# A two-layer diffusion trunk on one core: the modulation sums of the attention loop move to the output projections

## The chip, the core and the metric

The kernel runs on one core of one Trainium2 chip. The engines that matter are TensorE (PE, with its weight loads PEld), VectorE (DVE), ScalarE (ACT), GpSimd (POOL) and SyncE (SP), which issues nearly all DMAs. The metric is the device time of the whole kernel in microseconds (us), lower is better. Kernels are compared by the median of several runs; the trace is of one profiled execution.

## The reference

x is (512, 1024): 512 latent tokens; ctx is (256, 1024): context tokens; c is one conditioning vector. Two layers follow each other, all in fp32. For each layer, the modulation is a matrix-vector product

```
mods = silu(c) @ mod_w[layer] + mod_b[layer]     # 6 x 1024 values
h    = rms_norm(x, w_pre) * (1 + scale) + shift  # shift, scale from mods
x    = x + gate * rms_norm(mixer(h), w_post)     # gate from mods
h    = rms_norm(x, w_ffn_pre) * (1 + scale2) + shift2
x    = x + gate2 * rms_norm(ffn(h), w_ffn_post)
```

The mixer of layer 0 (hybrid) is a bidirectional chunked gated DeltaNet beside grouped-query attention of 8 heads over 768 keys (256 context, 512 latent), both from one input projection, and one output projection w_out (1024 x 1024). The mixer of layer 1 (short convolution) is an input projection, a gated depthwise convolution and again a 1024 x 1024 output projection. The feed-forward part is an up projection, a depthwise convolution, a gate and a down projection. Which part of mods is needed when: the first 2 x 1024 values before the first projection; the rest of layer 0 from its output projection on; those of layer 1 from the end of layer 0's feed-forward part on, with gates and feed-forward values from layer 1's output projection on.

## The kernel before

Activations lie transposed, channels in the 128 partitions and 512 tokens in the free dimension, as eight tiles x[:, c, :]. A weight is loaded in units of 256 columns (w_raw, 1 MB, two buffers); ACT copies it to a rounded high part (w_hi, `split_hi`), DVE subtracts to get the low part (w_lo, `split_lo`), and PE multiplies three times per k tile (high x high, high x low, low x high). A unit makes two output tiles of 128 channels. Each engine has a program of its own, written out in order in one function for each; semaphores are the only link between them. Nothing is scheduled by a planner, so an engine that waits holds up everything behind it in its list.

The modulation is computed on the side. The first 16 of 96 parts of 128 come from rows of mod_w by PE. The other 80 are 40 pairs of 256 columns, numbered j = 0 to 39 (`PAIRS`). For each pair SP loads 1 MB (8 k tiles of 256, `load_mod_pair`); ACT multiplies each k tile by silu(c) in place (`products`, eight activations); GpSimd adds the eight k tiles in three steps of 1024, 512 and 256 elements (`mod_parts`); PE sums over the partitions by two products with a vector of ones (`mod_columns`), each writing one column of a PSUM bank. Pairs 0 to 11 run in the input projection, 12 to 19 in the DeltaNet stage, 20 to 39 in the attention loop, two in every three steps (`mod_block`).

The attention loop has 32 steps i (8 heads x 4 query blocks of 128) and a few more to drain. PE: scores of step i (L937, L938) into one of two pairs of PSUM banks; transposes of the probabilities of step i-2 (L911) into banks 4 and 5, the only buffer of them; then, in three of four steps, a third of the values product of an earlier head (L922 to L924). ACT: copy of the transposed probabilities (PTh, L1379), exp (prob, L1393), products. DVE: row maximum, reciprocal, normalisation, and the low part of the transposed probabilities (PTl, L1924). At i = 32 ACT waits for all 40 pairs and splits the first two units of w_out, and DVE does the same. Their loads wait for the pairs too, since w_raw and the pairs' slots (`mraw_c`) share space.

Behind the loop DVE makes all norm weights (`norm_weights`). The output projection (`out_units`, `y_units`) has four units, tiles t = 0 to 7. PE does tiles 0 and 1 with the k tiles outermost, the others one after the other. Per tile ACT squares the PSUM result (sum_y, L1418) and the weighted y (sum_z, L1420), DVE makes y = PSUM x weight (L1955), y * x (L1958) and a running sum (L1961), GpSimd adds the squares. After tiles 1, 3 and 5 ACT and DVE split the next unit but one. Tile t writes PSUM bank t mod 4. The same functions do the second output projection, in layer 1.

## Time and profile before

| | us |
|---|---|
| median of 3 runs (lowest, highest) | 1708.76 (1706.11, 1711.48) |
| the profiled execution | 1714.39 |
| its span | 1712.6 |
| PE busy in the span | 1576.1 (92%) |
| DVE busy | 873.1 (51%) |
| ACT busy | 668.5 (39%) |
| GpSimd busy | 369.5 (22%) |
| ACT's products of pairs 12 to 39 (L1234, 224 instructions) | 92.2 |

The span is the time from the first to the last instruction of the profiled execution; the execution's own time is 1.8 us longer. The attention loop lies at 524 to 672 us of it, the first output projection at 692 to 740 us, the second at 1267 to 1315 us. The mean grant of the TensorE clock over the whole execution is 0.943 of full speed. The chain of work that ended last is PE for 77% of the span, DVE 10%, ACT 6%, GpSimd 3%.

### The profile page before, as it was taken

Reading aid. Unit: us, or ns where it says so; the run is one execution under the profiler, and the core shown is the slowest. Engines: PE = TensorE matmul, PEld = TensorE weight load, DVE = VectorE, ACT = ScalarE, POOL = GpSimd, SP = SyncE. Lnnn points to the kernel's source line nnn. Section 1 sums busy time; section 2 is a strip of 40 time slices with the busy share of each in tenths; the row PEclk is TensorE's granted clock in tenths of the full one; section 3 lists DMA queues with packets and bytes.
Section 4 is the critical chain, followed back from the end, with each engine's and each line's share of the span. In section 5 each row is a group of like instructions: output and inputs, shape, how many; then the busy total and the mean of one; then the engine's idle time right before and its main releaser. Section 6 shows DMA issues by size and latency. Waiting matters only on the chain.

```text
span 1712.6 us, 19828 instructions
## 1 busy us (share of the span) xinstructions
PE 1576.1 (92%) x7752; PEld 1290.8 (75%) x7752; DVE 873.1 (51%) x1150; ACT 668.5 (39%) x1044; POOL 369.5 (22%) x255
## 2 busy tenths in 40 slices
PE   8899896669978886999999999989999999999997
PEld 2688786568965554868888888868888788888886
DVE  2654424887626676574444434464446644444222
ACT  2444536313436896224333332232233433343221
POOL 3028502346764663300000001100003000000000
PEclk9899898789985998989999999999998999999999
DMA  8325610001133453213333222213222233232231
GB/s 337 99 86 172 172 50 13 1 1 50 50 113 109 148 172 77 71 50 99 98 98 98 95 90 92 95 47 111 92 92 74 74 99 98 98 98 92 83 96 50
DMA packets 153907, 160.18 MB, mean 94 GB/s; under 512 B 11383, under 2 KB 151144, under 8 KB 152808
## 3 DMA queue, kind: packets, MB, share of 16 engines
q1 hardware_dynamic: 153344, 158.95, 28.9%
q8 instruction: 52, 0.85, 0.2%
q10 hardware_dynamic: 488, 0.18, 0.0%
q14 instruction: 23, 0.19, 0.0%
HBM read 157.03 MB, written 2.10 MB: 93 GB/s over the span
## 4 chain that ended last, share of the span: by engine, by line
PE 77%; DVE 10%; ACT 6%; POOL 3%; issue 2%; DMA 1%; SPq 0%; DVEq 0%; ACTq 0%; POOLq 0%
PE ps L502 19%; PE ps L503 19%; PE ps L504 19%; ACT mod_raw_c L1234 2%; DVE blocks_inv L1746 2%; DVE sub_prod L1743 1%; PE ps L557 1%; POOL mod_raw_c L2144 1%; PE ps L954 1%; PE ps L956 1%; PE ps L955 1%; PE ps L726 1%; PE ps L911 1%; DVE w_lo L1534 1%; PE ps L615 1%
## 5 line engine op out<-in xcount | busy, mean ns | idle before, releaser
L1534 DVE TENSOR_TENSOR w_lo<-w_raw,w_hi 128x2048 fp32r<-128x2048 f32 x100 | 232.1, 2321 | 495.3 <-ACT w_hi L1180 495.3
L502 PE MATMUL ps<-h_hi,w_hi 128*128 128x512 f32 x968 | 380.0, 393 | 2.0 <-DVE w_lo L1534 2.0
L503 PE MATMUL ps<-h_lo,w_hi 128*128 128x512 f32 x968 | 379.5, 392 | 0.0
L504 PE MATMUL ps<-h_hi,w_lo 128*128 128x512 f32 x968 | 378.9, 391 | 0.0
L1180 ACT ACTIVATE w_hi<-w_raw 128x2048 fp32r<-128x2048 f32 x100 | 191.3, 1913 | 317.6 <-PE ps L504 272.3
L502 PEld LDWEIGHTS ps<-h_hi,w_hi 128*128 128x128 f32 x968 | 183.3, 189 | 40.5 <-DVE w_lo L1534 2.5
L504 PEld LDWEIGHTS ps<-h_hi,w_lo 128*128 128x128 f32 x968 | 183.4, 189 | 38.7
L503 PEld LDWEIGHTS ps<-h_lo,w_hi 128*128 128x128 f32 x968 | 183.2, 189 | 37.8
L2257 POOL TENSOR_TENSOR sum_acc_y<-sum_acc_y,sum_y 128x512 f32<-128x512 f32 x18 | 27.0, 1502 | 588.8 <-ACT sum_y L1418 588.8
L2144 POOL TENSOR_TENSOR mod_raw_c<-mod_raw_c 128x1024 f32<-128x1024 f32 (+2 forms) x84 | 127.2, 1515 | 70.2 <-ACT mod_raw_c L1234 65.7
L502 PE MATMUL ps<-mid_hi,w_hi 128*128 128x512 f32 x338 | 132.9, 393 | 0.0
L504 PE MATMUL ps<-mid_hi,w_lo 128*128 128x512 f32 x338 | 131.8, 390 | 0.0
L503 PE MATMUL ps<-mid_lo,w_hi 128*128 128x512 f32 x338 | 131.6, 389 | 0.0
L1234 ACT ACTIVATE mod_raw_c<-mod_raw_c,cvec 128x256 f32<-128x256 f32 x224 | 92.2, 500 | 4.2 <-DMA mod_raw_c<-in_mod_w 4.2
L2257 POOL TENSOR_TENSOR tmp<-tmp,tmp 128x512 f32<-128x512 f32 x6 | 7.8, 1297 | 380.7 <-ACT tmp L1414 380.7
L2144 POOL TENSOR_TENSOR mod_raw_e<-mod_raw_e 128x1024 f32<-128x1024 f32 (+1 forms) x24 | 57.5, 2394 | 88.4 <-ACT mod_raw_e L1234 87.4
L504 PEld LDWEIGHTS ps<-mid_hi,w_lo 128*128 128x128 f32 x338 | 63.4, 188 | 13.3
L503 PEld LDWEIGHTS ps<-mid_lo,w_hi 128*128 128x128 f32 x338 | 63.5, 188 | 12.9
L502 PEld LDWEIGHTS ps<-mid_hi,w_hi 128*128 128x128 f32 x338 | 63.5, 188 | 12.8
L1955 DVE TENSOR_SCALAR y<-ps,post_w 128x512 f32<-128x512 f32 x32 | 23.9, 748 | 68.4 <-ACT tmp L1414 30.3
L1458 ACT ACTIVATE mid_hi<-tmp 128x512 f32 (+1 forms) x44 | 27.1, 633 | 66.7 <-DVE tmp L2055 66.7
L1453 ACT ACTIVATE tmp<-tmp 128x512 f32<-128x512 f32 x44 | 27.8, 632 | 62.7 <-DVE tmp L2039 62.2
(347 smaller groups left out, 2688.5 us busy)
## 6 DMA issues: line engine op xcount, KB each, us to landing
w_raw<-in_ffn_w_up SPq DMA_DIRECT2D x44, 1024.0 KB, 5.1
mod_raw_c<-in_mod_w SPq DMA_DIRECT2D x28, 1024.0 KB, 5.4
w_raw<-in_ffn_w_down SPq DMA_DIRECT2D x16, 896.0 KB, 4.8
mod_raw_e<-in_mod_w SPq DMA_DIRECT2D x12, 1024.0 KB, 5.2
w_raw<-in_sc_w_in SPq DMA_DIRECT2D x12, 1024.0 KB, 5.2
w_raw<-in_hyb_w_in SPq DMA_DIRECT2D x9, 1024.0 KB, 7.7
mod_raw_a<-in_mod_w SPq DMA_DIRECT2D x8, 1024.0 KB, 16.2
w_raw<-in_ffn_w_down SPq DMA_DIRECT2D x8, 1024.0 KB, 5.1
```

The source lines that it names most:

```text
L502: mm(dst, hi, xh[:, k0 + k, :], start=first and k == 0, stop=False)
L503: mm(dst, hi, xl[:, k0 + k, :], start=False, stop=False)
L504: i = mm(dst, lo, xh[:, k0 + k, :], start=False, stop=last and k == nk - 1)
L1180: nc.scalar.activation(whi[s][:, :], raw[s][:, :], ACT.Copy).then_inc(sem("w_hi"), 1)
L1234: i = nc.scalar.activation(slot[:, k, :], slot[:, k, :], ACT.Copy, scale=cvec[:, k, 0:1])
L1453: nc.scalar.activation(tmp[2 * par + r][:, :], tmp[2 * par + r][:, :], ACT.Silu).then_inc(sem("sg"), 1)
L1458: nc.scalar.activation(mid_hi[:, bass.ds(2 * i + (2 * j0 + r), 1), :].rearrange("p c t -> p (c t)"), tmp[2 * par + r][:, :], ACT.Copy).the ...
L1534: V.tensor_tensor(wlo[s][:, :], raw[s][:, :], f32(whi[s][:, :]), ALU.subtract).then_inc(sem("w_lo"), 1)
L1746: V.tensor_tensor(x[:, 0:j + 1, j + 1:B32], x[:, 0:j + 1, j + 1:B32], p, ALU.subtract).then_inc(sem("elim"), 1)
L1955: V.tensor_scalar(y[:, t, :], b, pw, None, ALU.mult).then_inc(sem("yev"), 1)
L2144: G.tensor_tensor(dst, a, b, ALU.add).then_inc(sem("mod_acc"), 1)
L2257: G.tensor_tensor(a[:, :], a[:, :], q[t % 2][:, :], ALU.add).then_inc(sem("ya"), 1)
```

## The change

Pairs 20 to 39 leave the attention loop. Ten (20 to 29) go to the first output projection, ten (30 to 39) to the second. In each projection two pairs belong to each of tiles 0 to 4 (`late_at`). Three things follow each other for a pair of tile t: ACT's products, in the list of the unit of tile t behind its split; the three adds, now on DVE, behind DVE's work on tile t+1 (`late_adds`); the columns on PE, ahead of the matmuls of tile t+3 (`mod_columns(late_at(j // 2, t - 3))`). The pairs have six slots in a region that is free then (`mraw_l`), four of them used in the second projection. Pair 20 is loaded when gT has been used, 21 after the last scores, 22 and on after the last values product; later pairs when the adds have freed their slot. The first two splits of w_out move from step 32 to steps 10 and 20, and these units are loaded ahead of the loop. The norm weights are made in three parts: for layer 0 behind the loop, for layer 1 in each projection behind tile 6 (`later_weights`). Some semaphores are merged. GpSimd has no pair left after the DeltaNet stage.

```diff
@@ -118,6 +118,8 @@
+        mraw_l = [view(region(f"mod_raw_l{i}", KC * UW, 32 + 8 * i), "p (k n) -> p k n", n=UW) for i in range(6)]
+        lsum = view(region("late_sums", 8 * UW, 80), "p (j n) -> p j n", n=UW)
@@ -203,14 +205,37 @@
+        LATE = EARLY + LEVEL_PAIRS
+        LATE_HALF = (PAIRS - LATE) // 2
...
-            return (j - EARLY) % 2 if j < EARLY + LEVEL_PAIRS else (0, 1, 3, 4, 5)[(j - EARLY - LEVEL_PAIRS) % 5]
+            if j < LATE:
+                return (j - EARLY) % 2
+            i = j - LATE
+            return i % 6 if i < LATE_HALF else 2 + (i - LATE_HALF) % 4
...
+        def late_at(half, t):
+            j0 = LATE + LATE_HALF * half
+            return [j for j in range(j0, j0 + LATE_HALF) if (j - j0) // 2 == t]
...
+        def late_sums(j):
+            return 3 * (j - LATE + 1)
@@ -381,14 +401,19 @@
-                if users:
+                if users and users[-1] >= LATE:
+                    sp.wait_ge(sem("late"), late_sums(users[-1]))
+                elif users:
                     sp.wait_ge(sem("mod_done"), 2 * (users[-1] + 1))
-                elif s in (3, 4):
-                    sp.wait_ge(sem("Z"), 4 * NT)
-                elif s == 5:
-                    sp.wait_ge(sem("o"), 8)
-                    sp.wait_ge(sem("S"), 2 * NT - 2)
-                sp.dma_start(mraw_c[s][:, :, :], mod_source(j)).then_inc(sem(f"mod_in{s}"), 16)
+                if j == LATE:
+                    sp.wait_ge(sem("on"), 2 * HEADS)
+                if j == LATE + 1:
+                    sp.wait_ge(sem("sc"), A_HEADS * SEQ // P)
+                if j == LATE + 2:
+                    sp.wait_ge(sem("pv"), A_HEADS)
+                if j == LATE + LATE_HALF:
+                    sp.wait_ge(sem("tile"), 2 * U_SCIN)
+                sp.dma_start(slot_tile(j)[:, :, :], mod_source(j)).then_inc(sem(f"mod_in{s}"), 16)
@@ -441,13 +466,20 @@
-            for j in range(EARLY, PAIRS):
+            for j in range(EARLY, LATE):
                 load_mod_pair(j)
-            sp.wait_ge(sem("mod_done"), 2 * PAIRS)
+            sp.wait_ge(sem("mod_done"), 2 * LATE)
+            sp.wait_ge(sem("o"), 8)
             load_wout(12)
             load_wout(13)
+            for j in range(LATE, LATE + 4):
+                load_mod_pair(j)
             load_wout(14)
+            for j in range(LATE + 4, LATE + 6):
+                load_mod_pair(j)
             load_wout(15)
+            for j in range(LATE + 6, LATE + LATE_HALF):
+                load_mod_pair(j)
@@ -481,8 +513,12 @@
+            for j in range(LATE + LATE_HALF, LATE + LATE_HALF + 4):
+                load_mod_pair(j)
             sqb(sc_in, U_SCIN + 8)
             sqb(sc_out, U_SCOUT)
+            for j in range(LATE + LATE_HALF + 4, PAIRS):
+                load_mod_pair(j)
@@ -517,16 +553,19 @@
                         if k == KC - 1 and names[r]:
                             i.then_inc(sem(names[r]), 1)
-            def mod_column(m, acc):
-                mm(bank(7, 1, 16 + m), acc, ones[:, 0:1], start=True, stop=True).then_inc(sem("mod_done"), 1)
+            def mod_column(b, m, acc):
+                mm(bank(b, 1, 16 + m), acc, ones[:, 0:1], start=True, stop=True).then_inc(sem("mod_done"), 1)
             def mod_columns(pairs):
                 for j in pairs:
-                    pe.wait_ge(sem("mod_acc"), acc_c(j))
-                    acc = macc[:, j % 6, :] if j < EARLY else mraw_c[slot_of(j)][:, 0, :]
+                    if j < LATE:
+                        pe.wait_ge(sem("mod_acc"), acc_c(j))
+                    else:
+                        pe.wait_ge(sem("late"), late_sums(j))
+                    acc = macc[:, j % 6, :] if j < EARLY else slot_tile(j)[:, 0, :] if j < LATE else lsum[:, (j - LATE) % 8, :]
                     for part in range(2):
-                        mod_column(16 + 2 * j + part, acc[:, part * P:(part + 1) * P])
+                        mod_column(column_bank(j), 16 + 2 * j + part, acc[:, part * P:(part + 1) * P])
             def sum_columns(sq, idx, n, first, last):
@@ -940,7 +979,6 @@
                     turn(i - 2)
                 if i >= 6 and (i - 6) % NQ < 3:
                     values((i - 6) // NQ, (i - 6) % NQ)
-                mod_columns(mod_block(i, 3))
             tcol = lambda r: (lambda w, k: w[slot[0]][:, k, r * P:(r + 1) * P])
@@ -1042,6 +1080,7 @@
                         continue
                     for r in range(2):
                         t = 2 * u + r
+                        mod_columns(late_at(j // 2, t - 3))
                         bank_free(j, t)
                         if t < KC - 1:
                             i = mm3(bank(b0 + t % 4), tcol(r), KC, mix_hi, mix_lo, s)
@@ -1394,13 +1433,8 @@
                                          bias=stat[:, 32 + i:33 + i], accum_out=stat[:, 64 + i:65 + i]).then_inc(sem("expd"), 1)
                 if i >= 9 and (i - 9) % NQ == 0:
                     head_hi((i - 9) // NQ)
-                for j in mod_block(i, 0):
-                    act.wait_ge(sem(f"mod_in{slot_of(j)}"), landed(j))
-                    products(mraw_c[slot_of(j)])
-                if i == A_HEADS * NQ:
-                    act.wait_ge(sem("mod_done"), 2 * PAIRS)
-                    split_hi(U_WOUT, 0)
-                    split_hi(U_WOUT + 1, 1)
+                if i in (10, 20):
+                    split_hi(U_WOUT + i // 20, i // 20)
             act.wait_ge(sem("norm_w"), 2)
@@ -1426,6 +1460,10 @@
                         y_squares(j, 2 * u + r)
                     if u < 3:
                         split_hi(u0 + u + 2, u % 2)
+                    for t in (2 * u, 2 * u + 1):
+                        for jj in late_at(j // 2, t):
+                            act.wait_ge(sem(f"mod_in{slot_of(jj)}"), landed(jj))
+                            products(slot_tile(jj))
@@ -1880,22 +1918,54 @@
                     for d in range(2):
                         finished(k + 2 + d)
                         decayed_keys(k + 2 + d)
+            def vec_part(l, m, n, b):
+                V.tensor_tensor(modv[:, l, m:m + n, 0], bank(b, n, 16 + MODS * l + m), vec[:, 1, MODS * l + m:MODS * l + m + n],
+                                ALU.add).then_inc(sem("modv"), 1)
+            def post_weights(k, l, m, row):
+                return V.tensor_tensor(post_w[:, k, :], modv[:, l, m * KC:(m + 1) * KC, 0], vec[:, 0, row:row + KC], ALU.mult)
+            m1, m2 = 2 * (LATE - MODS // 2 + 8), 2 * (LATE + LATE_HALF - MODS // 2 + 8)
             def norm_weights():
-                dve.wait_ge(sem("mod_done"), 2 * PAIRS)
-                V.tensor_tensor(modv[:, 0, 16:MODS, 0], bank(7, MODS - 16, 32), vec[:, 1, 16:MODS], ALU.add).then_inc(sem("modv"), 1)
-                V.tensor_tensor(modv[:, 1, :, 0], bank(7, MODS, 16 + MODS), vec[:, 1, MODS:2 * MODS], ALU.add).then_inc(sem("modv"), 1)
+                dve.wait_ge(sem("mod_done"), 2 * LATE)
+                vec_part(0, 16, MODS - 16, 7)
+                vec_part(1, 0, m1, 7)
                 dve.wait_ge(sem("modv"), 3)
                 pre_weights(1, 0, 4 * KC, 0, V_FFNPRE)
-                pre_weights(2, 1, KC, 0, V_MIXPRE + KC)
-                pre_weights(3, 1, 4 * KC, 0, V_FFNPRE + KC)
-                for k, l, m, row in ((0, 0, 2, V_MIXPOST), (1, 0, 5, V_FFNPOST), (2, 1, 2, V_MIXPOST + KC), (3, 1, 5, V_FFNPOST + KC)):
-                    i = V.tensor_tensor(post_w[:, k, :], modv[:, l, m * KC:(m + 1) * KC, 0], vec[:, 0, row:row + KC], ALU.mult)
-                i.then_inc(sem("norm_w"), 1)
+                post_weights(0, 0, 2, V_MIXPOST)
+                post_weights(1, 0, 5, V_FFNPOST).then_inc(sem("norm_w"), 1)
+            def later_weights(half):
+                dve.wait_ge(sem("mod_done"), 2 * (LATE + LATE_HALF * (half + 1)))
+                vec_part(1, m2 if half else m1, MODS - m2 if half else m2 - m1, 1 if half else 5)
+                dve.wait_ge(sem("modv"), 4 + half)
+                if half:
+                    pre_weights(3, 1, 4 * KC, 0, V_FFNPRE + KC)
+                    post_weights(3, 1, 5, V_FFNPOST + KC).then_inc(sem("norm_w"), 1)
+                else:
+                    pre_weights(2, 1, KC, 0, V_MIXPRE + KC)
+                    post_weights(2, 1, 2, V_MIXPOST + KC).then_inc(sem("norm_w"), 1)
+            def late_adds(j):
+                t, n = slot_tile(j), late_sums(j) - 3
+                dve.wait_ge(sem("mod_prod"), j - EARLY // 2 + 1)
+                V.tensor_tensor(t[:, 0:4, :], t[:, 0:4, :], t[:, 4:8, :], ALU.add).then_inc(sem("late"), 1)
+                dve.wait_ge(sem("late"), n + 1)
+                V.tensor_tensor(t[:, 0:2, :], t[:, 0:2, :], t[:, 2:4, :], ALU.add).then_inc(sem("late"), 1)
+                dve.wait_ge(sem("late"), n + 2)
+                if j >= LATE + 8:
+                    dve.wait_ge(sem("mod_done"), 2 * (j - 7))
+                V.tensor_tensor(lsum[:, (j - LATE) % 8, :], t[:, 0, :], t[:, 1, :], ALU.add).then_inc(sem("late"), 1)
             dve.wait_ge(sem("gate"), HEADS)
             dve.wait_ge(sem("osd"), 1)
             V.reciprocal(odev[:, :], odev[:, :]).then_inc(sem("orc"), 1)
-            dve.wait_ge(sem("Vah"), 1)
+            dve.wait_ge(sem("osd"), 2)
             V.tensor_tensor(Vl[:, :, :].rearrange("p n t -> p (n t)"), bank(4, ALL),
                                 f32(Vh[:, :, :]).rearrange("p n t -> p (n t)"), ALU.subtract).then_inc(sem("Va"), 1)
             for h in range(HEADS):
@@ -1942,9 +2012,8 @@
                     turn_lo(i - 2)
                 if i >= 9 and (i - 9) % NQ == 0:
                     head_lo((i - 9) // NQ)
-                if i == A_HEADS * NQ:
-                    split_lo(U_WOUT, 0)
-                    split_lo(U_WOUT + 1, 1)
+                if i in (10, 20):
+                    split_lo(U_WOUT + i // 20, i // 20)
             norm_weights()
@@ -1964,9 +2033,14 @@
                 for u in range(4):
                     for r in range(2):
                         dve.wait_ge(sem("tile"), 2 * (u0 + u) + r + 1)
-                        y_tile(j, 2 * u + r)
-                    if u < 3:
-                        split_lo(u0 + u + 2, u % 2)
+                        t = 2 * u + r
+                        y_tile(j, t)
+                        if t == KC - 2:
+                            later_weights(j // 2)
+                        if r and u < 3:
+                            split_lo(u0 + u + 2, u % 2)
+                        for jj in late_at(j // 2, t - 1):
+                            late_adds(jj)
             def boundary(j, u, pre, hb, shift):
@@ -2246,8 +2320,6 @@
-            for j in range(EARLY + LEVEL_PAIRS, PAIRS):
-                mod_parts(j)
```

The change writes the order of instructions out anew. On ACT, in the first output projection, from the squares of tile 0 on, the list before reads (sum_acc_y, sum_y: squares of the PSUM result; sum_acc_z, sum_z: squares of y; w_hi0, w_hi1: splits of w_out's units):

```order
L1418 ACTIVATE sum_acc_y_77<-ps 128x512
L1420 ACTIVATE sum_acc_z_78<-y_80 128x512
L1418 ACTIVATE sum_y1_72<-ps 128x512
L1420 ACTIVATE sum_z1_74<-y_80 128x512
L1180 ACTIVATE w_hi0_61<-w_raw0_59 128x2048
L1418 ACTIVATE sum_y0_71<-ps 128x512
L1420 ACTIVATE sum_z0_73<-y_80 128x512
```

and now:

```order
L1452 ACTIVATE sum_acc_y_77<-ps 128x512
L1454 ACTIVATE sum_acc_z_78<-y_80 128x512
L1452 ACTIVATE sum_y1_72<-ps 128x512
L1454 ACTIVATE sum_z1_74<-y_80 128x512
L1219 ACTIVATE w_hi0_61<-w_raw0_59 128x2048
L1273 ACTIVATE mod_raw_l0_110<-mod_raw_l0_110,cvec_53 128x256 x8
L1273 ACTIVATE mod_raw_l1_111<-mod_raw_l1_111,cvec_53 128x256 x8
L1273 ACTIVATE mod_raw_l2_112<-mod_raw_l2_112,cvec_53 128x256 x8
L1273 ACTIVATE mod_raw_l3_113<-mod_raw_l3_113,cvec_53 128x256 x8
L1452 ACTIVATE sum_y0_71<-ps 128x512
L1454 ACTIVATE sum_z0_73<-y_80 128x512
L1452 ACTIVATE sum_y1_72<-ps 128x512
```

Four pairs' products (mod_raw_l0 to l3) stand between the split of unit 2 and the squares of tile 2. Four more follow the split of unit 3, and two the split after that.

On DVE, from the y of tile 1 on, the list before reads (y: PSUM x weight; sum_x and tmp3: y * x and its running sum; w_lo0: the low part of unit 2):

```order
L1955 TENSOR_SCALAR y_80<-ps,post_w_55 128x512
L1958 TENSOR_TENSOR sum_x1_76<-y_80,x_50 128x512
L1961 TENSOR_TENSOR tmp3_68<-tmp3_68,sum_x1_76 128x512
L1534 TENSOR_TENSOR w_lo0_63<-w_raw0_59,w_hi0_61 128x2048
L1955 TENSOR_SCALAR y_80<-ps,post_w_55 128x512
L1958 TENSOR_TENSOR sum_x0_75<-y_80,x_50 128x512
L1961 TENSOR_TENSOR tmp3_68<-tmp3_68,sum_x0_75 128x512
```

and now:

```order
L2024 TENSOR_SCALAR y_80<-ps,post_w_55 128x512
L2027 TENSOR_TENSOR sum_x1_76<-y_80,x_50 128x512
L2030 TENSOR_TENSOR tmp3_68<-tmp3_68,sum_x1_76 128x512
L1572 TENSOR_TENSOR w_lo0_63<-w_raw0_59,w_hi0_61 128x2048
L1957 TENSOR_TENSOR mod_raw_l0_110<-mod_raw_l0_110 128x1024
L1959 TENSOR_TENSOR mod_raw_l0_110<-mod_raw_l0_110 128x512
L1963 TENSOR_TENSOR late_sums_116<-mod_raw_l0_110 128x256
L1957 TENSOR_TENSOR mod_raw_l1_111<-mod_raw_l1_111 128x1024
L1959 TENSOR_TENSOR mod_raw_l1_111<-mod_raw_l1_111 128x512
L1963 TENSOR_TENSOR late_sums_116<-mod_raw_l1_111 128x256
L2024 TENSOR_SCALAR y_80<-ps,post_w_55 128x512
L2027 TENSOR_TENSOR sum_x0_75<-y_80,x_50 128x512
```

The adds of pairs 0 and 1 of the projection (mod_raw_l0, l1; the result in late_sums) stand ahead of the y of tile 2. Adds of this kind were on GpSimd's list before.

## Rows read from the trace of the kernel before

**Rows 1.** Windows view of every engine: us, busy us (instructions) of each, PEclk, DMA share, GB/s.

```profile
670.00:692.00 22.00, 8.70 (x30) 6.58 (x29) 7.10 (x5) 5.46 (x6) 0.00 (x0) 0.69 0.76 185
...
702.00:740.00 38.00, 37.06 (x179) 30.88 (x177) 29.84 (x25) 16.02 (x20) 18.46 (x12) 1.00 0.26 83
...
527.00:670.00 143.00, 127.19 (x512) 85.00 (x511) 97.78 (x164) 118.82 (x261) 90.84 (x60) 0.83 0.35 112
```

**Rows 2.** Timeline of ACT in the loop: start us, us, engine, line, operation; last the idle before.

```profile
648.69 0.81 ACT L1379 ACTIVATE PTh<-ps 128x768 fp32r<-128x768 f32 x1 [1.14 <-PE ps L911]
...
650.27 3.29 ACT L1234 ACTIVATE mod_raw_c<-mod_raw_c,cvec 128x256 f32<-128x256 f32 x8
653.47 0.79 ACT L1379 ACTIVATE PTh<-ps 128x768 fp32r<-128x768 f32 x1
```

**Rows 3.** Timeline of PE in the loop, TensorE clock at 2.4 GHz, and its last scores.

```profile
650.30 1.12 PE L937 MATMUL ps<-ak,aq 64*128 64x512 f32 x2
...
651.78 0.87 PE L911 MATMUL ps<-const,prob 128*128 128x128 f32 x6
652.41 0.48 PE L922 MATMUL ps<-PTh,Vh 128*128 128x512 f32 x1
...
653.89 0.50 PE L522 MATMUL ps<-const,mod_raw_c 128*128 128x1 f32 x4
654.32 1.12 PE L937 MATMUL ps<-ak,aq 64*128 64x512 f32 x2
...
664.07 1.12 PE L937 MATMUL ps<-ak,aq 64*128 64x512 f32 x2
```

**Rows 4.** Timeline of PE, 549 to 565 us, clock at 1.2 GHz.

```profile
549.15 2.07 PE L937 MATMUL ps<-ak,aq 64*128 64x512 f32 x2
...
555.91 0.85 PE L522 MATMUL ps<-const,mod_raw_c 128*128 128x1 f32 x4
556.69 2.07 PE L937 MATMUL ps<-ak,aq 64*128 64x512 f32 x2
...
564.21 1.12 PE L937 MATMUL ps<-ak,aq 64*128 64x512 f32 x2
```

**Rows 5.** Timeline of ACT, DVE and PE at the loop's end.

```profile
669.43 0.81 ACT L1379 ACTIVATE PTh<-ps 128x768 fp32r<-128x768 f32 x1 [1.26 <-PE ps L911]
...
670.27 0.96 DVE L1924 TENSOR_TENSOR PTl<-ps,PTh 128x768 fp32r<-128x768 f32 x1 [1.15 <-ACT PTh L1379]
...
671.38 0.85 PE L911 MATMUL ps<-const,prob 128*128 128x128 f32 x6 [0.58 <-DVE PTl L1924]
684.95 0.77 PE L922 MATMUL ps<-PTh,Vh 128*128 128x512 f32 x1 [12.72 <-DVE mix_lo L1931]
```

**Rows 6.** Timeline of PE, then ACT, in the first output projection.

```profile
691.70 0.39 PE L1037 MATMUL ps<-mix_hi,w_hi 128*128 128x512 f32 x1
...
702.16 0.60 ACT L1418 ACTIVATE sum_acc_y<-ps 128x512 f32<-128x512 f32 x1 [9.67 <-PE ps L1039]
...
706.23 1.90 ACT L1180 ACTIVATE w_hi<-w_raw 128x2048 fp32r<-128x2048 f32 x1
...
737.01 0.60 ACT L1418 ACTIVATE sum_y<-ps 128x512 f32<-128x512 f32 x1 [4.71 <-PE ps L1007]
```

**Rows 7.** Timeline of DVE in the first output projection.

```profile
703.68 0.69 DVE L1958 TENSOR_TENSOR tmp<-y,x 128x512 f32<-128x512 f32 x1
704.90 0.75 DVE L1955 TENSOR_SCALAR y<-ps,post_w 128x512 f32<-128x512 f32 x1 [0.53 <-ACT sum_y L1418]
...
706.75 1.67 DVE L1961 TENSOR_TENSOR tmp<-tmp,sum_x 128x512 f32<-128x512 f32 x1
708.35 2.28 DVE L1534 TENSOR_TENSOR w_lo<-w_raw,w_hi 128x2048 fp32r<-128x2048 f32 x1
```

**Rows 8.** Timeline of ACT, last tile of the second output projection.

```profile
1277.72 0.60 ACT L1418 ACTIVATE sum_acc_y<-ps 128x512 f32<-128x512 f32 x1 [3.92 <-PE ps L1039]
...
1312.62 0.60 ACT L1418 ACTIVATE sum_y<-ps 128x512 f32<-128x512 f32 x1 [4.71 <-PE ps L1007]
```

19 lines of the change are left out of this document (10 added, 9 removed).

## The prediction

> **What bounds the kernel now.** I read the windows view of the attention loop first, then one engine's timeline after another inside it, then the same for the first output projection. In the loop, 527 to 670 us, TensorE (PE) is busy 127.19 of 143 us and ScalarE (ACT) 118.82 [rows 1]. PE's share flatters it, since part of that is at the 1.2 GHz clock level (mean grant 0.83). At 2.4 GHz one loop step in which ACT has a modulation pair lasts as long as ACT's own list: from the copy PTh at 648.69 to the next at 653.47 are 4.78 us, of which the eight products take 650.27 to 653.47, 3.2 us [rows 2]. PE needs less: scores to scores 654.32 - 650.30 = 4.02 us, 0.43 of it the two pair columns, so 3.59 without them [rows 3]. So the products on ACT set the period there, and removing them should let PE set it. After the loop PE stands idle for 12.72 us, because the first two weight splits of the output projection are ahead of the last probability copy on ACT and DVE [rows 5]. In the output projection the picture is the reverse: PE is busy 37.06 of 38 us, ACT 16.02, DVE 29.84 [rows 1].
>
> **What the change takes away in the loop.** I call the steps of the loop i = 0 to 31.
> - Steps 8 to 31: their scores start at 564.21 [rows 4] and 664.07 [rows 3], 99.86 us for 23 steps. Afterwards 17 of them hold a third of a values product and cost PE 3.59; 6 have none and are bounded by the one PSUM buffer of the transposed probabilities: 0.85 (L911) + 0.84 (PTh 669.43 to PTl 670.27) + 1.11 (PTl to the next L911) = 2.80 us [rows 5]. 17 x 3.59 + 6 x 2.80 = 77.8.
> - Into this stretch come the two splits, one at i = 10 and one at i = 20. Each is 1.90 on ACT [rows 6] and then 2.28 on DVE [rows 7], with the next row maximum queued behind it. Hidden by PE's own work they cost 0, fully exposed 4.2; I take 3 each, nearer the exposed end because DVE has under a microsecond of slack in a step of 3.59. 77.8 + 6 = 83.8, so 16.1 us are saved.
> - Steps 0 to 7 run at 1.2 GHz, where PE is the bound already: 549.15 to 556.69 is 7.54, of which 0.78 are columns [rows 4]. Four pairs' columns go, 3.1 us, and a little waiting of the steps without values; I take 4. If the clock rises one step sooner, it is 8; below 3 it can't fall.
> - The end: L911 of the last step starts at 671.38, the last head's values at 684.95 [rows 5], 13.57 later. Without the splits between them there remain 0.85 + 0.84 + 0.96 and the low part of the head before, about 3.6: 10.0 saved. The 18 values matmuls now run at 1.2 GHz after the idle time, 684.95 to 691.70 = 6.75 [rows 5, 6]; at 2.4 GHz they are one and a half steps less, 4.1. I take 2 of these 2.65.
> Sum 4 + 16.1 + 10.0 + 2 = 32.1 us, bounds 24 and 41. The sum is against the profiled execution (1714.39, span 1712.6); the median of the runs is 1708.76, and I carry the difference over to that.
> VectorE's row maximum and normalisation lose GpSimd as a neighbour. That shortens DVE, but DVE isn't the bound above, so I count it at nothing.
>
> **What it adds in each projection.** Ten pairs: 80 products on ACT at 3.2 us a pair [rows 2], 32 us; 30 adds on DVE; 20 columns on PE; ten loads. DVE's adds are not in this trace; from 512 elements at 0.69 and 2048 at 2.28 [rows 7], 1024, 512 and 256 elements are 1.22 + 0.69 + 0.42, with three issue gaps about 2.4 us a pair. The lowest reading is proportion to 2048, 2.0; the highest takes the 1.67 that L1961 needs for 512 elements beside GpSimd in place of 0.69 [rows 7], 5.8 if every add met it. GpSimd is busy 18.46 of 38 us there [rows 1], so half of them at most: 4.1.
> The point is the order, not the total. ACT queues four pairs behind the split of unit 2, ahead of the squares of tile 2; DVE queues two pairs' adds behind each tile; and PE waits for the sums of two pairs ahead of each of tiles 3 to 7. I set time 0 at the projection's first matmul (691.70). Before, ACT's first square is at +10.5, its split at +14.5, its last square at +45.3 [rows 6].
> - ACT: split to +16.4, four pairs to 19.6, 22.8, 26.0, 29.2. DVE has the sums of pairs 0 and 1 at +25.3. PE, done with tile 2 at +16.3, waits for them 9 us, then does tile 3.
> - Squares of tile 2 at +29.2; DVE's work on a tile is 708.35 - 704.90 = 3.45 [rows 7], to +33.4, then two sums to +38.2: tile 4 starts 38.7.
> - The second square of tile 3 waits for y (+39), so the next split is at +39.6 to 41.5 and DVE is through its half at 43.9. Pairs 4 to 7 at 44.7, 47.9, 51.1, 54.3; sums of 4 and 5 at +50.4: tile 5 starts 50.9.
> - Squares of tile 4 only at +54.3; y to 58.5, sums of 6 and 7 to 63.3: tile 6 starts 63.8. Next split 66.6, pairs 8 and 9 to 73.0, sums at +75.5: tile 7 starts 76.0.
> - From there to the last square are 7.0 us as before: +83.0 for +45.3, 37.7 us later.
> PE is now idle 6 to 9 us before each of five tiles. After 12.7 us of idleness its next 18 matmuls ran at 1.2 GHz and cost 2.65 more [rows 5, 6]. For tiles 3 to 6 a slow tile (24 matmuls, 10.3 us) still ends before ACT asks for it; only tile 7 lies on the path: +2.6, bounds 0 and 4.9. The second projection has the same order and the same length (first square to last 34.9 us in both [rows 6, 8]). So 40.3 us each, bounds 33 (adds at 2.0, no slow clock, the first square of a tile not held up) and 49 (adds at 4.1).
> Loads: pairs 2 and 3 wait for the last values and stand before the weights of unit 2 on SyncE's queue, which ACT wants at +14.5; 3 MB are due in that time. I take 0, the bound is 2 us. The later ones wait for sums that come 10 us or more before ACT asks.
> Sum: 2 x 40.3 - 32.1 = 48.5, so 1708.8 + 48.5 = 1757 us.
>
> **Rivals.**
> 1. The order does not matter and ACT simply fills its idle time: 16.02 + 32 = 48 us after +10.5, so the projection ends at about +58 where ACT's window ended at +48; 10 us each, 20 - 32 = -12, 1697 us, faster. For it: ACT is idle 22 of 38 us [rows 1]. Against it: the squares of tile 2 are queued behind four pairs, and PE waits for sums. It decides if PE's wait before tile 3 is under about 3 us.
> By the Trainium skill (Perfetto Trace Analysis, Optimization Strategy) performance "may be improved" by interleaving stages whose busiest engines differ; by that rule alone this is the outcome. The rows agree that the busiest engines differ, and leave open whether the work interleaves.
> 2. The adds run at 4.1 us a pair because GpSimd adds squares beside them. Five of the ten pairs' adds lie on the path (2, 3, 6, 7, 9), 5 x 1.7 = 8.5 us a projection: 1774. For it: L1961 at 1.67 against L1958 at 0.69 [rows 7]. Against: most of GpSimd's two adds a tile are over when the sums start.
> The Trainium skill (SBUF — State Buffer, SBUF: two separate sides) calls the pair of ports an exclusive lock for a VectorE operation with two SBUF inputs against a GpSimd one; the L1961 rows agree in direction.
> 3. The loop's gain is smaller: the waits between ACT, DVE and PE that rows 5 show (1.26, 1.15 and 0.58 us in one step) keep a step at about 3.9 in place of 3.4; 0.5 x 24 = 12 us of the 32 stay away: 1769.
> 4. The projections hide more than I think (PE waits shorter, tiles at 2.4 GHz): 28 us each, 1733.
>
> **How the numbers follow.** Forecast 1757: 0.64. Rival 1: 0.05. Rival 2: 0.12. Rival 3: 0.09. Rival 4: 0.08. Remaining 0.02 no change: it needs the gain and cost to cancel, which no case above does. With bounds 24 to 41 against 66 to 98 the sum is between +25 and +74, 1734 to 1783; I give 1732 to 1780, which leaves rival 1 out. A measurement of this kernel tells about 0.3%, 5 us, from no change. Faster 0.05, same 0.02, slower 0.93.
>
> **What would show it.** Right: loop steps of 3.4 to 3.6 us at 2.4 GHz and no idle time over 4 us ahead of the last values; in the projections PE idle before each of tiles 3 to 7 with the columns released by DVE's adds, the last square some 38 us later than before. Wrong: PE idle in the projection under 15 us in all; or loop steps still over 4 us; or the split of unit 2 waiting for its weights, which would add a cost that I have at nothing.

## The result, and the profile after

| | before | after |
|---|---|---|
| median of the runs (lowest, highest), us | 1710.12 (1706.11, 1714.17), 4 runs | 1767.45 (1763.64, 1772.89), 4 runs |
| after : before | | 1.0327, 95% interval 1.0298 to 1.0356 |
| the profiled execution, its span | 1714.39, 1712.6 | 1772.89, 1771.1 |
| mean clock grant | 0.943 | 0.929 |

The changed kernel is slower by 57 us; 1757 was forecast, with 1732 to 1780 as the range. The profiled execution of after is the slowest of its four runs.

The page of the changed kernel, busy time and one group (line, engine, operation, count, then busy us, mean ns, then idle time before it and who ended it):

```profile
PE 1603.0 (91%) x7752; PEld 1306.8 (74%) x7752; DVE 916.9 (52%) x1212; ACT 669.8 (38%) x1044; POOL 275.1 (16%) x195
...
L558 PE MATMUL ps<-const,late_sums 128*128 128x1 f32 x80 | 17.2, 319 | 46.6 <-DVE late_sums L1963 46.6
```

ACT does the same 670 us as before, GpSimd 94 less, DVE 44 more. PE has the same matmuls, but stands 46.6 us ahead of the pairs' columns, waiting for DVE's third addition.

The windows view (columns as in rows 1) of the first projection, then of the loop:

```profile
672.00:749.00 77.00, 53.72 (x200) 43.12 (x198) 54.25 (x56) 45.58 (x98) 16.92 (x12) 0.78 0.46 140
527.00:661.00 134.00, 119.30 (x454) 72.89 (x454) 93.83 (x169) 62.41 (x105) 0.00 (x0) 0.88 0.04 12
```

Against [rows 1] ACT's share in the loop falls from 118.8 of 143 us to 62.4 of 134. In the projection nobody is full: PE 70%, DVE 70%, ACT 59%, at a grant of 0.78.

The loop on PE: the scores of step 8 and, at 2.4 GHz, of three steps in a row; the step after the second split; the scores of step 31; the last head's values product; and the projection's first matmul:

```profile
556.59 1.12 PE L976 MATMUL ps<-ak,aq 64*128 64x512 f32 x2
...
584.93 1.12 PE L976 MATMUL ps<-ak,aq 64*128 64x512 f32 x2
...
588.62 1.12 PE L976 MATMUL ps<-ak,aq 64*128 64x512 f32 x2
...
592.31 1.12 PE L976 MATMUL ps<-ak,aq 64*128 64x512 f32 x2
...
608.95 1.12 PE L976 MATMUL ps<-ak,aq 64*128 64x512 f32 x2
...
613.99 0.84 PE L950 MATMUL ps<-const,prob 128*128 128x128 f32 x6 [3.48 <-DVE PTl L1994]
...
617.27 1.57 PE L976 MATMUL ps<-ak,aq 64*128 64x512 f32 x2
...
646.74 1.12 PE L976 MATMUL ps<-ak,aq 64*128 64x512 f32 x2
...
657.61 0.47 PE L961 MATMUL ps<-PTh,Vh 128*128 128x512 f32 x1 [2.71 <-DVE mix_lo L2001]
...
661.77 0.39 PE L1075 MATMUL ps<-mix_hi,w_hi 128*128 128x512 f32 x1
```

A step with values takes 3.69 us (4.02 before, in [rows 3], and 4.78 where ACT had a pair, in [rows 2]); the 12.72 us of idle time ahead of the last values [rows 5] are 2.71. At the second split PE stands 3.48 us, and that step lasts 8.32 us.

ACT's timeline in the first projection, and the first and last square of the second:

```profile
672.23 0.60 ACT L1452 ACTIVATE sum_acc_y<-ps 128x512 f32<-128x512 f32 x1 [9.67 <-PE ps L1077]
...
676.29 1.90 ACT L1219 ACTIVATE w_hi<-w_raw 128x2048 fp32r<-128x2048 f32 x1
678.10 12.86 ACT L1273 ACTIVATE mod_raw_l<-mod_raw_l,cvec 128x256 f32<-128x256 f32 x32
690.87 0.57 ACT L1452 ACTIVATE sum_y<-ps 128x512 f32<-128x512 f32 x1
...
701.46 0.63 ACT L1454 ACTIVATE sum_z<-y 128x512 f32<-128x512 f32 x1 [4.64 <-DVE y L2024]
...
748.91 0.60 ACT L1452 ACTIVATE sum_y<-ps 128x512 f32<-128x512 f32 x1 [8.32 <-PE ps L1045]
...
1295.78 0.60 ACT L1452 ACTIVATE sum_acc_y<-ps 128x512 f32<-128x512 f32 x1 [3.92 <-PE ps L1077]
...
1372.84 0.60 ACT L1452 ACTIVATE sum_y<-ps 128x512 f32<-128x512 f32 x1 [8.86 <-PE ps L1045]
```

First to last square are 76.7 and 77.1 us where they were 34.9 and 34.9 [rows 6, 8]. The squares of tile 2 stand behind 12.86 us of products. DVE's timeline of one pair, and PE's columns of both pairs ahead of tile 3 and of the second pair ahead of tile 7:

```profile
681.41 1.23 DVE L1957 TENSOR_TENSOR mod_raw_l<-mod_raw_l 128x1024 f32<-128x1024 f32 x1 [0.73 <-ACT mod_raw_l L1273]
682.67 0.69 DVE L1959 TENSOR_TENSOR mod_raw_l<-mod_raw_l 128x512 f32<-128x512 f32 x1
683.40 0.42 DVE L1963 TENSOR_TENSOR late_sums<-mod_raw_l 128x256 f32<-128x256 f32 x1
```

```profile
683.88 1.01 PE L558 MATMUL ps<-const,late_sums 128*128 128x1 f32 x4 [5.62 <-DVE late_sums L1963]
687.07 1.01 PE L558 MATMUL ps<-const,late_sums 128*128 128x1 f32 x4 [2.18 <-DVE late_sums L1963]
...
739.32 1.01 PE L558 MATMUL ps<-const,late_sums 128*128 128x1 f32 x4 [3.53 <-DVE late_sums L1963]
```

All of these waits in the first projection, by the view of waits (us in total, times, longest):

```profile
PE ps L558 <- DVE late_sums L1963: 23.3, 9, 5.6
```

Where the 58.5 us between the two profiled executions lie, by marks on ACT's timeline: first exponential of the loop, first square of a projection, and first h_hi (the high part of the next stage's input) behind its boundary. The boundary is the stretch from a projection's last square to there, in which PE sums the squares and the norm is applied:

| stretch, us | before | after | difference |
|---|---|---|---|
| loop: first exponential to first square | 174.5 | 145.0 | -29.5 |
| first projection and its boundary | 46.5 | 90.3 | +43.8 |
| from there to the second projection | 529.1 | 533.3 | +4.2 |
| second projection and its boundary | 48.5 | 89.1 | +40.6 |

The 4.2 us in the third line are mostly clock: 3.1 of them lie between the last square and the first h_hi of the second boundary (the one inside this stretch, behind layer 0's feed-forward part), 13.5 us for 10.4, where PE's sums over the partitions take 1.84 us a group instead of 1.05. The windows view of PE over it (busy us, count, PEclk, DMA share, GB/s), of after and then of before over the same work, 15 us earlier:

```profile
1125.00:1150.00 25.00, 22.94 (x98) 0.73 0.13 43
1150.00:1175.00 25.00, 22.85 (x90) 0.93 0.13 43
```

```profile
1110.00:1135.00 25.00, 20.95 (x107) 0.93 0.13 43
1135.00:1160.00 25.00, 24.32 (x101) 1.00 0.17 51
```

Why the grant fell there isn't shown. In the kernels below that leave this stretch as it was, it took between 1.0 us less and 3.1 more than before.

### The profile page after: what moved, and what is told of

Read it like the earlier page. It is cut to its first block, busy times and chain, and to the rows that moved or that the text cites. A ratio compares the mean times of both kernels' runs of the same rounds, so it can differ in the third digit from the quotient of the medians.

```text
span 1771.1 us, 19844 instructions
## 1 busy us (share of the span) xinstructions
PE 1603.0 (91%) x7752; PEld 1306.8 (74%) x7752; DVE 916.9 (52%) x1212; ACT 669.8 (38%) x1044; POOL 275.1 (16%) x195
## 4 chain that ended last, share of the span: by engine, by line
PE 75%; DVE 12%; ACT 7%; POOL 3%; issue 2%; DMA 1%; SPq 0%; DVEq 0%; ACTq 0%; POOLq 0%
PE ps L538 17%; PE ps L539 17%; PE ps L540 17%; ACT mod_raw_l L1273 4%; DVE blocks_inv L1784 2%; PE ps L976 2%; DVE sub_prod L1781 1%; PE ps L950 1%; POOL mod_raw_c L2218 1%; PE ps L992 1%; PE ps L596 1%; PE ps L1014 1%; PE ps L994 1%; PE ps L993 1%; ACT w_hi L1219 1%
## 5 line engine op out<-in xcount | busy, mean ns | idle before, releaser
L538 PEld LDWEIGHTS ps<-h_hi,w_hi 128*128 128x128 f32 x968 | 183.0, 189 | 40.3 <-DVE w_lo L1572 2.3
L540 PEld LDWEIGHTS ps<-mid_hi,w_lo 128*128 128x128 f32 x338 | 63.4, 188 | 13.5
L539 PEld LDWEIGHTS ps<-mid_lo,w_hi 128*128 128x128 f32 x338 | 63.5, 188 | 12.8
L538 PEld LDWEIGHTS ps<-mid_hi,w_hi 128*128 128x128 f32 x338 | 63.5, 188 | 12.8
L1273 ACT ACTIVATE mod_raw_l<-mod_raw_l,cvec 128x256 f32<-128x256 f32 x160 | 64.5, 493 | 0.0
L558 PE MATMUL ps<-const,late_sums 128*128 128x1 f32 x80 | 17.2, 319 | 46.6 <-DVE late_sums L1963 46.6
L558 PEld LDWEIGHTS ps<-const,late_sums 128*128 128x128 f32 x80 | 15.7, 275 | 51.2 <-DVE late_sums L1963 37.7
L1496 ACT ACTIVATE mid_hi<-tmp 128x512 f32 (+1 forms) x44 | 27.1, 633 | 66.7 <-DVE tmp L2129 66.7
```

The lines of the kernel that those rows point to most:

```text
L538: mm(dst, hi, xh[:, k0 + k, :], start=first and k == 0, stop=False)
L539: mm(dst, hi, xl[:, k0 + k, :], start=False, stop=False)
L540: i = mm(dst, lo, xh[:, k0 + k, :], start=False, stop=last and k == nk - 1)
L558: mm(bank(b, 1, 16 + m), acc, ones[:, 0:1], start=True, stop=True).then_inc(sem("mod_done"), 1)
L1273: i = nc.scalar.activation(slot[:, k, :], slot[:, k, :], ACT.Copy, scale=cvec[:, k, 0:1])
L1496: nc.scalar.activation(mid_hi[:, bass.ds(2 * i + (2 * j0 + r), 1), :].rearrange("p c t -> p (c t)"), tmp[2 * par + r][:, :], ACT.Copy).the ...
```

## The experiments

The question was what makes a pair cost 4 us in a projection where PE was the bound before and ACT idle 22 of 38 us: the order (what is queued behind what), the columns' wait on PE, or the lists of ACT and DVE as such. Ten kernels ran; each row gives the median and its ratio to before on the same chip, and the marks of its trace: loop as in the table above, then first to last square of the two projections. prod1, add1, work_out and small_pool leave work out, the other six do all of it. The diffs are cut to the lines that matter; "..." marks where.

| kernel | us | ratio (95%) | loop | projection 1 | projection 2 |
|---|---|---|---|---|---|
| prod1 | 1749.2 | 1.020 (1.014, 1.027) | 145.0 | 66.3 | 65.4 |
| add1 | 1742.6 | 1.017 (1.010, 1.023) | 145.0 | 63.5 | 65.0 |
| work_out | 1718.6 | 1.002 (0.999, 1.005) | 145.3 | 46.1 | 55.5 |
| cols_last | 1763.3 | 1.029 (1.021, 1.036) | 145.2 | 75.1 | 75.0 |
| inter | 1753.5 | 1.025 (1.020, 1.029) | 145.0 | 64.9 | 66.7 |
| inter_lag | 1753.9 | 1.022 (1.019, 1.026) | 145.1 | 59.1 | 63.8 |
| small_pool | 1750.4 | 1.022 (1.018, 1.025) | 145.4 | 70.5 | 70.3 |
| split_lag | 1766.5 | 1.031 (1.028, 1.034) | 141.4 | 76.8 | 76.2 |
| best | 1695.4 | 0.991 (0.988, 0.994) | 148.6 | 34.8 | 37.2 |
| best_lag | 1695.5 | 0.990 (0.987, 0.992) | 143.8 | 34.9 | 37.2 |

**prod1: one of eight products.**

```diff
-            def products(slot):
+            def products(slot, k0=0):
...
-                for k in range(KC):
+                for k in range(k0, KC):
...
-                            products(slot_tile(jj))
+                            products(slot_tile(jj), KC - 1)
```

> As the change, but ScalarE multiplies only the last of the eight k tiles of each of the twenty late pairs (the other seven products are left out, so the modulation is not the reference's). Theory A (ScalarE's and VectorE's lists are two bounds one behind the other; without the products VectorE's own work, 8 x 3.45 + 10 x 2.4 + 3 x 2.3 = 58.5 us from +11 us on, becomes the bound): last square of a projection at +69 us after its first matmul in place of +87, 18 us less in each, 1731 us. Theory B (ScalarE's 32 us are the whole cost): the projection is back near +50, 37 us less in each, 1693 us. Theory C (the adds on VectorE alone are the cost): no change, 1767 us.

Measured: the projections 10.4 and 11.7 us shorter where theory A wanted 18, 1749 instead of 1731. About 28 us of products went from ACT's list and only 10 to 12 came back: most of the products lay beside something else that was just as long.

**add1: the last of the three additions alone.**

```diff
-                V.tensor_tensor(t[:, 0:4, :], t[:, 0:4, :], t[:, 4:8, :], ALU.add).then_inc(sem("late"), 1)
-                dve.wait_ge(sem("late"), n + 1)
-                V.tensor_tensor(t[:, 0:2, :], t[:, 0:2, :], t[:, 2:4, :], ALU.add).then_inc(sem("late"), 1)
-                dve.wait_ge(sem("late"), n + 2)
...
-                V.tensor_tensor(lsum[:, (j - LATE) % 8, :], t[:, 0, :], t[:, 1, :], ALU.add).then_inc(sem("late"), 1)
+                V.tensor_tensor(lsum[:, (j - LATE) % 8, :], t[:, 0, :], t[:, 1, :], ALU.add).then_inc(sem("late"), 3)
```

> As the change, but VectorE makes only the last of the three adds of each of the twenty late pairs (the adds over 1024 and 512 elements are left out, so the modulation is not the reference's). Theory A: ScalarE's order stays the bound; last square at +76 us in place of +87, 11 us less in each projection, 1745 us. Theory B (ScalarE's products are the whole cost): no change beyond 2 us, 1765 us. Theory C (VectorE alone): back near +50, 1693 us.

Measured: 13.2 and 12.1 us shorter, 1743, near theory A (11 and 1745). The two additions took 12.2 + 8.8 = 21.0 us in the first projection of after, so 21 us of DVE's list are worth more than 28 us of ACT's. Theories B and C are out by both runs.

**work_out: both edits together.**

> As the change, with both left out: one product in eight and one add in three for each late pair (not the reference's modulation); the loads, the waits and the columns stay. Theory A: the rest, VectorE's list with the small adds ahead of each tile, ends a projection at +54 us in place of +45 before and +87 with the change; 1701 us. Rival D (the columns' waits on TensorE and its slow clock after them are a cost of their own, whatever the work): the projection stays above +65, over 1722 us. The loop is as in the change, some 30 us shorter than before.

Measured: 46.1 and 55.5 us, 30.6 and 21.6 shorter than after; in the first projection that is more than the two apart (23.6), in the second less (23.8). So neither list alone is the cost. 11.2 us of the first projection's 41.8 stay with little work left in the pairs: PE waits 4.8 us for sums, the columns themselves take 5.1, and the grant is 0.96. The kernel, 1719, missed theory A's 1701, most of it in the second projection, where some 43 were expected; there ACT waited 3.7 us for weights that stood behind the last pairs' loads, and 8.3 us for PE before the squares of tile 3.

**cols_last: the columns of eight pairs ahead of tile 7 only, the last two pairs' behind it.**

```diff
-                        mod_columns(late_at(j // 2, t - 3))
+                        if t == KC - 1:
+                            mod_columns([p for q in range(4) for p in late_at(j // 2, q)])
...
+                mod_columns(late_at(j // 2, 4))
```

> As the change, but TensorE makes the columns of the first eight late pairs ahead of tile 7 and those of the last two behind it, in place of two pairs ahead of each of tiles 3 to 7; the norm weights follow tile 7. Same work, same result. Theory A (the lists of ScalarE and VectorE hold the projection up, and TensorE's waits only show it): ScalarE's last products are still at +73, so the last square comes at +79 in place of +87, 8 us less in each projection, 1750 us. Rival D (TensorE's waits for the columns are the cost): the projection is back near +55, 1703 us.

Measured: only 1.6 and 2.1 us, 1763. Rival D (1703) is out, but theory A had wanted 8 us and 1750. PE's waits moved. Its waits in the first projection, this kernel (start us, us, operation, idle before):

```profile
704.57 0.80 PE L538 MATMUL ps<-mix_hi,w_hi 128*128 128x512 f32 x1 [11.73 <-DVE w_lo L1574]
722.44 1.01 PE L558 MATMUL ps<-const,late_sums 128*128 128x1 f32 x4 [7.64 <-DVE late_sums L1965]
...
740.89 1.86 PE L1014 MATMUL ps<-const,tmp 128*128 128x1 f32 x8 [9.25 <-DVE tmp L2032]
```

In after PE had waited 23.3 us for the columns' sums. Without that it waits 11.7 us for the low half of unit 3's weights (the split stands behind the same products and sums), then for the sums again, then for the running sum of tile 6. ACT's last products do end at +74 after the first matmul, as theory A had it; the running sum of tile 6, which PE also needs, stands behind DVE's last sums, and theory A had left that out. The column is where the wait shows, not what it costs.

**inter: one pair behind each tile.** ACT takes two pairs ahead of tile 0, one behind each tile's squares (two behind tile 3); DVE's sums go with them.

```diff
+        AFTER_TILE = {-1: (0, 1), 0: (2,), 1: (3,), 2: (4,), 3: (5, 6), 4: (7,), 5: (8,), 6: (9,), 7: ()}
...
-                        mod_columns(late_at(j // 2, t - 3))
+                        mod_columns(columns_at(j // 2, t))
```

> The changed kernel with the same work in another order: in both projections ScalarE takes two pairs' products ahead of the first tile and then one pair behind each tile's squares (two behind the fourth), in place of two pairs behind every unit; VectorE's sums go with them; the split of the next unit stands ahead of the products; the columns stand three tiles behind and the last five pairs' after tile 7. Nothing is added or left out. If the lists of ScalarE and VectorE bound the projection (my theory after the first runs), what counts is the length of the longer list: VectorE's is 8 x 3.45 (tile) + 8 x 2.4 (sums) + 3 x 2.3 (splits) = 53.7 us from the first tile on, so the first to the last square takes 52 to 58 us instead of 76.7 and 77.1, and the kernel 1767 - 2 x 20 = about 1727. If each pair costs some 4 us wherever it stands (it is work that nothing hides), the projections keep 75 us and the kernel 1765. If ScalarE alone counted, 48 us: 1709.

Measured: 64.9 and 66.7 us, neither the 52 to 58 of DVE's list nor the 75 of a fixed price, and 1753 instead of 1727. The timelines of ACT and of DVE in one tile say why:

```profile
679.66 0.63 ACT L1461 ACTIVATE sum_z<-y 128x512 f32<-128x512 f32 x1 [3.63 <-DVE y L2034]
...
689.39 0.63 ACT L1461 ACTIVATE sum_z<-y 128x512 f32<-128x512 f32 x1 [3.62 <-DVE y L2034]
689.92 3.29 ACT L1280 ACTIVATE mod_raw_l<-mod_raw_l,cvec 128x256 f32<-128x256 f32 x8
693.12 0.58 ACT L1459 ACTIVATE sum_y<-ps 128x512 f32<-128x512 f32 x1
697.33 0.63 ACT L1461 ACTIVATE sum_z<-y 128x512 f32<-128x512 f32 x1 [3.63 <-DVE y L2034]
```

```profile
693.25 1.22 DVE L1967 TENSOR_TENSOR mod_raw_l<-mod_raw_l 128x1024 f32<-128x1024 f32 x1 [1.32 <-ACT mod_raw_l L1280]
694.51 1.67 DVE L1969 TENSOR_TENSOR mod_raw_l<-mod_raw_l 128x512 f32<-128x512 f32 x1
696.21 0.43 DVE L1973 TENSOR_TENSOR late_sums<-mod_raw_l 128x256 f32<-128x256 f32 x1
696.55 0.75 DVE L2034 TENSOR_SCALAR y<-ps,post_w 128x512 f32<-128x512 f32 x1
```

One tile is 697.33 - 689.39 = 7.94 us, and the chain through both engines is as long: square of y 0.63, products 3.29, sums 1.22 + 1.67 + 0.43, y 0.75 (8.0 in all). Each engine waits for the other once a tile: DVE for products begun a moment before, ACT for y behind the sums. Two in-order lists with a handover in both directions add up; they don't overlap. DVE's running sum and its half of a split lie beside the products. ACT's half of a split does not: the tile before this one, with a split of 1.91 us ahead of its products, took 689.39 - 679.66 = 9.73 us.

**inter_lag: DVE's sums one tile behind.**

```diff
-                        for jj in late_at(j // 2, t):
+                        for jj in late_at(j // 2, t - 1):
                             late_adds(jj)
```

> The kernel with one pair behind each tile (last job), with one thing moved: VectorE's sums of a pair stand one tile behind ScalarE's products of it. In that kernel VectorE waited 14.8 us in the first projection for products just begun, while ScalarE waited 3.6 us per tile for y behind the sums: one chain y 0.75, square 0.63, products 3.3, sums 3.3 = 8.0 us per tile that goes through both engines. If that chain sets the pace, it is broken now and VectorE's own list is next: per tile 0.75 + 0.69 + 1.83 + 1.23 + 1.66 + 0.42 + 1.15 of a split = 7.7 us, two extra pairs 6.6: first to last square 58 to 63 us instead of 64.9 and 66.7, kernel 1741 to 1751 (before at 1714). If the chain didn't matter, 65 to 67 and 1753. If ScalarE's list were the bound, 50.

Measured: first to last square 59.1 and 63.8, as the chain theory wants (58 to 63; the second is just outside). DVE is busy 9.9 of 10 us in both windows from 680 to 700, so there its own list is the bound:

```profile
680.00:690.00 10.00, 8.18 (x32) 6.32 (x31) 9.86 (x8) 7.37 (x16) 3.73 (x3) 0.83 1.05 292
690.00:700.00 10.00, 8.34 (x41) 6.72 (x40) 9.86 (x9) 7.65 (x16) 2.60 (x2) 1.00 0.70 229
```

Later it isn't all: DVE waits 2.3 and 3.1 us for squares that stand behind ACT's products, and over the 59 us it is busy 52.6. The kernel as a whole gained nothing: 1753.9 and 1753.5 (1741 to 1751 was expected), and the first h_hi comes at 749.8 instead of 750.6. What the squares gained, the columns and sums over the partitions left over behind tile 7 took (last square to h_hi 20.3 us, 15.5 in inter, 11.6 before), at a grant of 0.51 from 720 to 750. The expectation had no term for them.

**small_pool: GpSimd's sums of squares on 4 columns in both projections.**

```diff
+                    w = 4 if j in (0, 2) else SEQ
-                    G.tensor_tensor(a[:, :], a[:, :], q[t % 2][:, :], ALU.add).then_inc(sem("ya"), 1)
+                    G.tensor_tensor(a[:, 0:w], a[:, 0:w], q[t % 2][:, 0:w], ALU.add).then_inc(sem("ya"), 1)
...
-                        G.tensor_tensor(acc_z[:, :], acc_z[:, :], qz[t % 2][:, :], ALU.add).then_inc(sem("ya"), 1)
+                        G.tensor_tensor(acc_z[:, 0:w], acc_z[:, 0:w], qz[t % 2][:, 0:w], ALU.add).then_inc(sem("ya"), 1)
```

> The changed kernel, but in both output projections GpSimd's additions into the running sums of squares take 4 columns instead of 512 (so these statistics are left out; all else stays). If VectorE's operations are slow beside GpSimd's (the running sum of xz 1.74 us instead of 0.69, the second addition of a pair 0.88 instead of 0.69, the third 0.53 instead of 0.42, xz 0.83 instead of 0.69), 6.3 + 1.9 + 1.1 + 1.0 = 10.3 us of VectorE's list go in each projection: first to last square about 66 to 70 us instead of 76.7 and 77.1, kernel 1747 to 1754 (before 1710 to 1714). If those operations are as long as they are without GpSimd's work beside them, or if VectorE's length isn't what counts, 75 to 77 and 1765. GpSimd's half of the port story priced high (rival 2 of the prediction) would want more than 10.

Measured: 70.5 and 70.3, 6.2 and 6.8 us shorter, just above the 66 to 70 expected; the kernel 1750, as expected. Some 10 us went from DVE's list, 6 to 7 came back. Groups of DVE in the first projection, of after and then of this kernel (busy us, mean ns):

```profile
L2030 DVE TENSOR_TENSOR tmp<-tmp,sum_x 128x512 f32<-128x512 f32 x6 | 10.5, 1743 | 0.2
L1959 DVE TENSOR_TENSOR mod_raw_l<-mod_raw_l 128x512 f32<-128x512 f32 x10 | 8.8, 880 | 0.3
```

```profile
L1959 DVE TENSOR_TENSOR mod_raw_l<-mod_raw_l 128x512 f32<-128x512 f32 x10 | 6.9, 692 | 0.3
...
L2030 DVE TENSOR_TENSOR tmp<-tmp,sum_x 128x512 f32<-128x512 f32 x6 | 4.3, 722 | 0.2
```

Contention with GpSimd is real (1743 to 722 ns, 880 to 692), but most of it is the running sum, which was at 1668 ns before the change too. What the moved pairs add through it in after is 10 x 0.19 + 10 x 0.11 (the third addition, 532 and 425 ns) + 6 x 0.08 = 3.5 us a projection.

**split_lag: the two low halves in the loop one step behind the high ones.**

```diff
-                if i in (10, 20):
-                    split_lo(U_WOUT + i // 20, i // 20)
+                if i in (11, 21):
+                    split_lo(U_WOUT + i // 21, i // 21)
```

> The changed kernel with one thing moved: VectorE's two low halves of the first projection's weights stand one step later in the attention loop (steps 11 and 21) than ScalarE's high halves (10 and 20), so that VectorE does not wait for ScalarE's split in the step in which it stands. If the loop's loss at the splits is that wait (PE idle 2.0 and 3.5 us there), the loop gets 2 to 4 us shorter in the trace (first square of the first projection at 668 to 670 us instead of 672.2) and the kernel about 1764. If it is the two operations' own length in the two lists (1.9 and 2.3 us), nothing changes: 672 and 1767.

Measured: the loop is 141.4 us instead of 145.0. The two splits gained unequally. Over the four steps around the first (14.4 us where there is no split), the changed kernel takes 17.7 us and this one 14.8: nearly all of that loss was DVE's wait within the step. Around the second they take 18.5 and 17.7: there the low half and a head's mix_lo stand together on DVE, PE still waits 1.73 us ahead of the transposes, and its matmuls behind that run at 1.2 GHz (0.63 us each instead of 0.40). The kernel's 1766.5 can't be told from 1767; the ratios, 1.031 and 1.033, overlap.

**best: sixteen pairs in the convolution stage.** The twelve units between the second boundary and the second output projection have PE at 131.00 of 131 us, DVE at 55.36, ACT at 38.27 (windows view of before):

```profile
1147.00:1278.00 131.00, 131.00 (x580) 108.51 (x579) 55.36 (x55) 38.27 (x39) 0.00 (x0) 1.00 0.30 97
```

There ACT and DVE have a unit's time, some 11 us, for each split. Pairs 20 to 23, whose sums are needed before that stage, stay in the loop as they were; the other sixteen go here, eleven among the convolution's units and five among the gate's, with three 1 MB slots.

```diff
+        LOOP_PAIRS = EARLY + LEVEL_PAIRS
+        LATE = LOOP_PAIRS + 4
+        FIRST = LATE + 11
...
+        def cx_pairs(b, part):
+            a = LATE + 3 * b
+            return [j for j in ((a,) if part == 0 else (a + 1, a + 2)) if j < FIRST]
...
+                    late_products(cx_pairs(i + j0, part))
...
+                for part in range(2):
+                    for jj in cx_pairs(i + j0, part):
+                        late_adds(jj)
...
+            pe.wait_ge(sem("scc"), KC)
+            mod_columns(range(LATE, FIRST))
             out_units(U_SCOUT, 2, "mix1", lambda k: k + 1)
```

> The kernel before with sixteen of the twenty pairs out of the attention loop and none in a projection: four pairs (20 to 23) stay in the loop's first steps, products on ScalarE and sums on GpSimd as before, the other sixteen have products on ScalarE and sums on VectorE among the twelve units of the short convolution's first matrix, where PE bounds and both engines wait for it; eleven pairs' columns stand on PE ahead of the second output projection and five inside it; the splits for the first projection stand in the loop as in the changed kernel. If the loop's gain is real and the loss is only that the projections had no room, the loop gives about 28 us, the first projection takes 35 us again, the convolution stage costs 0 to 6 and PE's columns 7: 1710 - 28 + 10 = 1692. If moved pairs cost 4 us each wherever they stand outside the loop, 16 x 4 = 64 come back: 1746.

Measured: 1695.4, ratio 0.991 (0.988 to 0.994): 0.9% less than before, a small gain, but one that the interval holds clear of 1. 1692 was expected; the loop gave 25.9 us instead of 28. The same stage in its trace, and the columns:

```profile
1121.00:1256.00 135.00, 135.00 (x612) 112.41 (x612) 89.39 (x103) 87.90 (x164) 0.00 (x0) 0.99 0.60 195
```

```profile
1239.38 4.97 PE L561 MATMUL ps<-const,late_sums 128*128 128x1 f32 x44
```

PE is never idle in it, though ACT does 50 us more and DVE 34; what the pairs cost is mostly their columns, 4.97 us for eleven pairs and 2.3 for the five inside the projection, 0.45 a pair. From the first projection's boundary to the second projection it takes 6.6 us more than before, and the second projection 2.3. The 4 us a pair of the alternative are refuted.

**best_lag: both.**

> The version with sixteen pairs in the convolution stage (last job, 1695 with before at 1714), and VectorE's two low halves in the loop one step later, as in the kernel with only that moved. There the loop took 141.4 us instead of 145.0; here 148.6 should become 145 and the kernel 1691 to 1692 (ratio 0.989). If the gain of the one doesn't add to the other, since the four pairs' products fill the loop's first steps, it stays at 1695 (0.991).

Measured: 1695.5, ratio 0.990 (0.987, 0.992); the loop took 143.8 us for 148.6, but the median shows nothing of it (1691 to 1692 was expected). In the profiled executions 5.7 us are lost again between the first projection's boundary and the second projection (541.5 us, 535.8 in best). 4.0 of them lie between last square and first h_hi of the second boundary, 14.4 us for 10.4, at a grant of 0.54. Whether that is chance these runs can't say.

## Why the prediction was right

**The loop: 32.1 forecast, 29.5 measured.** The total is closer than its terms:

| term of the loop, us | before | after | saved | forecast |
|---|---|---|---|---|
| first exponential to the scores of step 8 | 36.5 | 29.4 | 7.2 | 4 |
| scores of step 8 to those of step 31 | 99.9 | 90.2 | 9.7 | 16.1 |
| those to the last head's values | 20.9 | 10.9 | 10.0 | 10.0 |
| these to the projection's first matmul | 6.8 | 4.2 | 2.6 | 2 |

The end was right: PE's wait before the last values fell from 12.72 to 2.71. In steps 0 to 7 the clock rose one step sooner, for which the prediction had 8. The largest term was over-sized by 6.4 us. A step with values was forecast at 3.59 and is 3.69, just outside the 3.4 to 3.6 that it gave as a sign of being right; four steps without a split last 14.36 us where it counted 3 x 3.59 + 2.80 = 13.57, since PE waits for PTl (0.63 us) in the step behind the one without values. The splits, sized 3 us each, cost 3.3 and 4.1. So rival 3 had the mechanism (waits between ACT, DVE and PE), at 0.2 us a step instead of 0.5. That the total came out 2.6 off and not 6 is luck: the gain in steps 0 to 7 made up for half.

**The projections: 2 x 40.3 forecast, 41.8 and 42.2 measured** between first and last square. By the schedule of the prediction the sums of pairs 1, 3, 5, 7 and 9 are due at +25.3, +38.2, +50.4, +63.3 and +75.5 after the projection's first matmul (661.77 in after); they came at +25.2, +39.0, +51.0, +64.6 and +77.5. The last square stood at +83.0 plus 2.6 for a slow tile 7, and came at +87.1. One thing was off: PE was to be idle 6 to 9 us before each of five tiles; it waited 5.62 + 2.18 = 7.8 us before tile 3 and 2.6 to 4.8 before the others, 23.3 in all. The grant was 0.78 on the mean of that stretch, tiles 3 to 6 took 7.4 to 8.3 us instead of the 5.6 of tile 2, and the columns of each first pair ran inside the waits; together these make up the difference. As forecast, only the last tile lay on the path: from the last sum to the last square were 9.6 us, 7.0 + 2.6.

**What had no term.** The boundary behind the first projection took 2.0 us more (three of PE's five groups of sums at 1.2 GHz, 1.72 to 1.85 us instead of 1.03 to 1.34), the stretch with the second boundary 4.2, mostly clock. With 2.6 less gain in the loop and 3.4 more in the projections these are 12.2; the boundary behind the second projection took 1.6 less, and 0.6 lie outside the marks. That leaves 10.0, the difference between the 48.5 forecast and the 58.5 between the profiled executions. The median, 1767, is closer to rival 3's 1769 than to 1757; the terms that brought it there are these.

**The reason given, and what the runs showed.** The prediction said that "the point is the order, not the total". Little of that held. With its boundary the first projection took 46.5 us before, 90.3 after, 80.4 in inter and 79.5 in inter_lag; the second 48.5, 89.1, 84.6 and 83.9. So against the orders tried here the order as written costs 4.5 to 11 us, and these leave 33 to 36 of the 41 to 44; whether a still better one exists was not tried. What remains is mostly a total: on DVE 8 x 3.45 of tile work, 10 x 2.4 of sums and 3 x 2.3 of splits are 58.5 us where PE needs 35, and the chain through ACT and DVE is longer still. In inter_lag DVE is at that bound for part of the projection (9.86 of 10 us) and 89% busy over it. Rival 1 counted ACT's idle time alone, 22 of 38 us, and was never to be had: DVE was already busy 29.84 of 38 [rows 1], which leaves room for three pairs' sums.

The Trainium skill (Perfetto Trace Analysis, Optimization Strategy) says that performance may be improved by interleaving regimes whose busiest engine differs. The runs agree where the second engine has room too (best, 0.991) and not where it has none (after, 1.033).

**Rival 2, sums at 4.1 us through GpSimd.** They were 1.22 + 0.88 + 0.53 on the mean, 2.6 us, and small_pool takes 6 to 7 us from a projection with all of the contention, old and new. The Trainium skill (SBUF — State Buffer, SBUF: two separate sides) lets one of the two engines wait while the other has the ports; the trace agrees in direction, with 1743 ns beside GpSimd's work and 722 without.

**Loads at nothing** held: ACT split unit 2 of the first projection at 676.29 without a wait, and in the second, where four loads stood ahead of the weights, it waited for none in after. In work_out, with the pairs' work gone and the loads bunched, it did.

## What to carry to other kernels

Before work is moved into an engine's idle time, add up the list of every engine that touches it, in the stage that receives it, against the bound of that stage: here ACT had 22 us free, DVE 8, and the work needed 32 and 24. If it hands over from one in-order engine to a second that the first also waits for, the two times add up; letting the second run a step behind took 3 to 6 us off a projection's squares here, until its own list was full, and nothing off the kernel. Look for the stage in which the bound engine is full and both others are half empty: the same twenty pairs cost 84 us in two projections, and sixteen of them cost 9 around the convolution stage, 7 of it their columns. Check the terms of a sum as well as its total: here one was 6.4 us too large and another 3.2 too small.

## What was not expected of the hardware

- PE's clock fell with a pattern of short waits, not only after a long one: the grant was 0.78 over 77 us in which PE was busy 70%. Before tile 4 PE waited 2.40 and 1.66 us; the columns of the first pair took 0.58 us, those of the second 1.01, and the first matmuls of the tile 0.63 each instead of 0.39. Half of the pairs' columns took 1.01 us there, against 0.45 in best (4.97 for eleven).
- Which of DVE's additions is slow beside GpSimd depends on the order, and it is one at a time, longer by about 1 us: in inter the second of most pairs is at 1.63 to 1.67 instead of 0.69 and the others undisturbed, in inter_lag the third of half of the pairs at 1.37 to 1.51 instead of 0.42. GpSimd's operations beside them take 1.3 to 1.9 us.
- The same boundary (the second) runs at a mean grant between 0.73 and 0.93 in a window of 25 us around it from kernel to kernel, though its instructions are the same; from last square to first h_hi that is 10.4 to 14.4 us, up to 4 us of a total of 1700.
